# Expert weights on one core: expert 15 takes the third buffer after expert 2, and layer 0's first weights load earlier

## The reference, cut to what matters

```python
def moe(x, r_w, r_b, w1, w3, w2):
    ...
    for e in range(N_EXPERTS):
        h = jax.nn.silu(t @ w1[e]) * (t @ w3[e])
        out = out + gates[:, e:e + 1] * (h @ w2[e]).astype(jnp.float32)

for l in range(DEPTH):
    if l < N_A_LAYERS:
        mix, buf = conv_module(x, conv_past[l], ...)
        conv_new.append(buf)
    else:
        ...
    x = layer_norm(ALPHA * x + mix, ln_mix_g[l], ln_mix_b[l])
    x = layer_norm(ALPHA * x + moe(x, ...), ln_ffn_g[l], ln_ffn_b[l])
```

## Time and profile before

| what | before |
|---|---|
| median of 3 runs | 1090.54 us (1090.39 to 1094.48) |
| profiled execution | 1092.01 us, span 1090.4 us |
| mean granted TensorE clock | 0.936 of 2.4 GHz |
| TensorE busy | 960.4 us, 88% |
| VectorE, ScalarE, GpSimd busy | 338.4, 166.3, 105.3 us |
| moved by DMA | 266.96 MB, 245 GB/s over the span |
| chain that ended last | PE 68%, DMA 12%, DVE 9%, SPq 5% |

### The profile page before, as it was taken

The page is one execution under the profiler, slowest core; times in us unless marked ns, Lnnn a source line. Parts: engine busy times, 40 slices in busy tenths (PEclk is TensorE's granted clock), DMA queues, the critical chain, the costliest instruction groups (busy, mean ns, idle before and its releaser), DMA issues.

```text
span 1090.4 us, 14360 instructions
## 1 busy us (share of the span) xinstructions
PE 960.4 (88%) x4814; PEld 478.6 (44%) x4815; DVE 338.4 (31%) x806; ACT 166.3 (15%) x327; POOL 105.3 (10%) x198
## 2 busy tenths in 40 slices
PE   6979979899989998869998888889798999898993
PEld 4646535444333433326655555444543333333331
DVE  0945454522122211152224433212542121122115
ACT  1000032111111110011123322220111110111101
POOL 0260000101000000013000023000020000000000
PEclk9989989799989999998998989989789999899998
DMA  7974453999979999968203110458468499999981
GB/s 180 258 242 127 122 198 112 354 363 346 367 269 371 378 377 383 395 216 280 69 10 100 52 53 26 167 213 313 135 216 278 174 364 379 384 379 375 384 337 49
DMA packets 131654, 266.96 MB, mean 245 GB/s; under 512 B 7480, under 2 KB 39252, under 8 KB 131585
## 3 DMA queue, kind: packets, MB, share of 16 engines
q1 hardware_dynamic: 121200, 237.74, 62.0%
q10 hardware_dynamic: 5009, 16.15, 4.3%
q0 software_dynamic: 5392, 12.34, 4.1%
HBM read 259.78 MB, written 7.15 MB: 245 GB/s over the span
## 4 chain that ended last, share of the span: by engine, by line
PE 68%; DMA 12%; DVE 9%; SPq 5%; ACT 3%; issue 2%; DVEq 0%; ACTq 0%
PE bank L1004 17%; DMA w<-in_e_w 9%; PE bank L1012 7%; PE bank L897 4%; PE wide L1047 4%; SPq L420 3%; PE bank L788 3%; DMA dbuf<-in_a_w_pw 3%; PE wide L897 3%; PE wide L788 2%; PE wide L1787 2%; PE bank L951 2%; PE bank L804 2%; PE bank L1664 2%; PE bank L1765 2%
## 5 line engine op out<-in xcount | busy, mean ns | idle before, releaser
L1004 PE MATMUL bank<-w,dbuf 128*64 128x512 f32 x960 | 218.9, 609 | 16.4 <-DMA w<-in_e_w 14.9
L1004 PEld LDWEIGHTS bank<-w,dbuf 128*64 128x64 f32 x960 | 75.1, 140 | 155.2 <-issue 155.2
L1012 PE MATMUL bank<-w,dbuf 128*64 128x512 f32 x480 | 115.8, 626 | 11.0 <-DVE dbuf L1438 10.4
L1443 DVE COPY dbuf<-bank 64x512 f32<-64x512 f32 x64 | 44.1, 689 | 159.5 <-PE bank L1012 159.1
L1434 DVE TENSOR_TENSOR dbuf<-dbuf,bank 64x512 f32<-64x512 f32 x32 | 22.1, 690 | 205.1 <-ACT dbuf L707 205.1
L707 ACT ACTIVATE dbuf<-bank 64x512 f32<-64x512 f32 x32 | 18.9, 591 | 410.1 <-PE bank L1004 410.1
L1012 PEld LDWEIGHTS bank<-w,dbuf 128*64 128x64 f32 x480 | 38.6, 143 | 72.8 <-issue 72.8
L1047 PE MATMUL wide<-dbuf,ukT 128*128 128x512 f32 x128 | 62.9, 617 | 3.0 <-DVE dbuf L1443 3.0
L549 POOL COPY idx_col<-idx 64x1 int32 (+1 forms) x32 | 5.7, 179 | 555.6 <-PE bank L951 370.5
L951 PEld LDWEIGHTS bank<-ident,dbuf 64*128 64x128 f32 x448 | 38.9, 160 | 41.4 <-issue 36.8
L536 POOL DMA_DIRECT2D w<-in_cache_kpe x64 | 34.3, 536 | 224.4 <-PE bank L1765 120.6
(11 more groups left out here) (365 smaller groups left out, 1142.7 us busy)
## 6 DMA issues: line engine op xcount, KB each, us to landing
w<-in_e_w SPq DMA_DIRECT2D x90, 2048.0 KB, 20.4
dbuf<-in_a_w_pw SPq DMA_DIRECT2D x16, 512.0 KB, 7.2
w<-u_rows SPq DMA_DIRECT2D x32, 142.0 KB, 3.1
dbuf<-in_a_w_pw ACTq DMA_DIRECT2D x1, 4096.0 KB, 16.8
dbuf<-in_e_w SPq DMA_DIRECT2D x2, 2048.0 KB, 14.8
w<-in_cache_ckv SPq DMA_DIRECT2D x32, 128.0 KB, 2.6
dbuf<-in_cache_ckv SPq DMA_DIRECT2D x32, 128.0 KB, 2.2
dbuf<-in_b_w_o SPq DMA_DIRECT2D x2, 2048.0 KB, 8.5
```

The source lines that it names most:

```text
L1004: last = nc.tensor.matmul(bank[n * C:(n + 1) * C], x[:, k], w[n][k], start=(k == 0), stop=(k == KD - 1))
L1012: last = nc.tensor.matmul(bank[n * C:(n + 1) * C], h[:, k], w[k][:, n * 512:(n + 1) * 512], start=(k == 0), stop=(k == 3))
L1443: last = V.tensor_copy(y_pair[s * C:(s + 1) * C, h * 512:(h + 1) * 512], DOWN[h * C:(h + 1) * C, :])
```

## The change

Loads: the third buffer takes expert 15 as soon as expert 2 is done with it (`third_last`, between the loads of 4 and 5), in both layers; TensorE reads expert 15 from buffer 2 and the counts waited for follow. In layer 0 expert 2's w1 is issued once the gate products are done, the first matrix of expert 1 once the tails are transposed, its w2 once they are stored, all before the projection's end; its w3 and expert 2's dbuf part of w3 at the projection's end. The attention's first weights wait until expert 15's up product has read `dbuf`. Tails: transposed before the projection, in banks 2, 3, 6 and 7, packed by GpSimd after the last gate product, copied and stored by ScalarE behind the Silus; the projection of tiles 1 and 2 waits for those copies.

```diff
--- before.py
+++ after.py
@@ -101,7 +101,7 @@
     MISC = 9 * 16
     SHIFTS, GROUPS, STEPS = 4, 4, 8
     WC = SEQ + 4 * STEPS - 4
-    UB = [7, 4, 5, 7]
+    UB = [2, 3, 6, 7]
     ROUNDS_MAX = DEPTH * 2 * T // H
     OUT_STORES = 10
     PUT_ORDER = [(0, 0), (0, 1), (1, 0), (1, 1), (2, 0)]
@@ -415,25 +415,49 @@
                 src = a["e_w2"][l].rearrange("e (k p) d -> p e k d", p=P)[:, bass.ds(e, 1)]
                 return src.rearrange("p a k d -> p (a k) d")
 
+            def load_half(l, e, s, n):
+                sp.dma_start(part(w13[s], n * KD * FE, KD, FE), w13_rows(l, n, e)).then_inc(w13_ready[s], 16)
+
             def load_13(l, e, s):
                 for n in range(2):
-                    sp.dma_start(part(w13[s], n * KD * FE, KD, FE), w13_rows(l, n, e)).then_inc(w13_ready[s], 16)
+                    load_half(l, e, s, n)
 
             def load_2(l, e, s):
                 sp.dma_start(part(w2[s], 0, 4, D), w2_rows(l, e)).then_inc(w2_ready[s], 16)
 
-            def third_dbuf(l, n):
-                rows = w13_rows(l, n, 2)
+            def third_dbuf(l, n, e=2):
+                rows = w13_rows(l, n, e)
                 sp.dma_start(third_w3a if n else third_w1, rows[:, 0:5] if n else rows).then_inc(w13_ready[2], 16)
 
+            def third_xT(l, n, e=2):
+                if n == 0:
+                    sp.dma_start(third_w3b, w13_rows(l, 1, e)[:, 5:8]).then_inc(w13_ready[2], 16)
+                else:
+                    sp.dma_start(third_w2b, w2_rows(l, e)[:, 3:4]).then_inc(w2_ready[2], 16)
+
+            def third_tok(l, e=2):
+                sp.dma_start(third_w2a, w2_rows(l, e)[:, 0:3]).then_inc(w2_ready[2], 16)
+
             def third_rest(l):
-                w3, w2_all = w13_rows(l, 1, 2), w2_rows(l, 2)
                 sp.wait_ge(r_logit, 3 * (l + 1))
-                sp.dma_start(third_w3b, w3[:, 5:8]).then_inc(w13_ready[2], 16)
-                sp.dma_start(third_w2b, w2_all[:, 3:4]).then_inc(w2_ready[2], 16)
+                third_xT(l, 0)
+                third_xT(l, 1)
                 sp.wait_ge(x_stored, 48 * (l + 1))
                 sp.wait_ge(x_alpha, 3 * (l + 1))
-                sp.dma_start(third_w2a, w2_all[:, 0:3]).then_inc(w2_ready[2], 16)
+                third_tok(l)
+
+            def third_last(l):
+
+                served = sp.value_load(rounds[0:1, 2, 2:3], min_val=1, max_val=ROUNDS_MAX + 1)
+                sp.wait_ge(up_done, E * l + 3)
+                sp.wait_ge(m_up, served)
+                third_dbuf(l, 0, E - 1)
+                third_dbuf(l, 1, E - 1)
+                third_xT(l, 0, E - 1)
+                sp.wait_ge(down_done, E * l + 3)
+                sp.wait_ge(m_down, served)
+                third_xT(l, 1, E - 1)
+                third_tok(l, E - 1)
 
             def load_over(l, e, s, old):
 
@@ -449,25 +473,30 @@
                 sp.wait_ge(cnt_set, l + 1)
                 load_over(l, 3, 0, 0)
                 load_over(l, 4, 1, 1)
+                third_last(l)
                 with sp.Fori(0, (E - 6) // 2) as it:
                     for s in range(2):
                         e = it * 2 + s + 5
                         load_over(l, e, s, it * 2 + s + 3)
-                load_over(l, E - 1, 0, E - 3)
 
             load_13(0, 0, 0)
             load_2(0, 0, 0)
+            sp.wait_ge(h_done, KD)
+            third_dbuf(0, 0)
+            sp.wait_ge(u_turned, 4)
+            load_half(0, 1, 1, 0)
+            sp.wait_ge(u_stored, 32)
+            load_2(0, 1, 1)
             sp.wait_ge(mix_done, 3)
-            third_dbuf(0, 0)
+            load_half(0, 1, 1, 1)
             third_dbuf(0, 1)
-            sp.wait_ge(u_turned, 4)
-            load_13(0, 1, 1)
-            sp.wait_ge(u_stored, 32)
             sp.wait_ge(xg_ready[0], 16)
             sp.wait_ge(xg_ready[1], 16)
-            load_2(0, 1, 1)
             third_rest(0)
             load_rest(0)
+            served = sp.value_load(rounds[0:1, 2, E - 1:E], min_val=1, max_val=ROUNDS_MAX + 1)
+            sp.wait_ge(up_done, E)
+            sp.wait_ge(m_up, served)
             sp.dma_start(wkv[:, :, 0:KV], a["s_w_dkv"].rearrange("(k p) n -> p k n", p=P)).then_inc(ld_kv, 16)
             sp.dma_start(wkv[:, :, KV:], a["s_w_kr"].rearrange("(k p) n -> p k n", p=P)).then_inc(ld_kv, 16)
             sp.dma_start(wdq, a["b_w_dq"][0].rearrange("(k p) n -> p k n", p=P)).then_inc(ld_q, 16)
@@ -517,7 +546,6 @@
 
             pool.wait_ge(glu_done, KD)
             pool.wait_ge(state_set, 1)
-            pool.wait_ge(z_done, 1)
             nc.gpsimd.tensor_copy(u_samp.rearrange("p k (b s) -> p k b s", b=DB),
                                   ext_s[:, :, :, CS:EXTS])\
                 .then_inc(u_packed, 1)
@@ -629,6 +657,7 @@
                 act.wait_ge(nrm_done, j + 1)
                 nc.scalar.activation(acc[:, j], acc[:, j], ACT.Silu, scale=vec_T[:, 24 + j:25 + j],
                                      bias=vec_T[:, 32 + j:33 + j]).then_inc(z_done, 1)
+            copy_tails(act)
             act_experts(act, 0)
             act_attention(act)
             act_experts(act, 1)
@@ -688,8 +717,6 @@
                     nc.scalar.activation(xT[:, 4 * q:4 * q + 4, t0:t0 + m], src, ACT.Copy).then_inc(xT_copied, 1)
                 if i == 0:
                     act_norm(act, 2 * l, 2)
-                if i == 1 and l == 0:
-                    copy_tails(act)
             act.wait_ge(r_aff0, l + 1)
             for i, (t0, m) in enumerate(TILES):
                 act.wait_ge(r_logit, 3 * l + i + 1)
@@ -848,6 +875,7 @@
             conv(7)
             add_channels(6)
             add_channels(7)
+            turn_tails(pe)
             pe.wait_ge(pw2_ready, 16)
             pe_experts(pe, 0, acc, pw2, z_done)
             pe_attention(pe)
@@ -868,6 +896,7 @@
 
         def turn_tails(pe):
 
+            pe.wait_ge(glu_done, KD)
             for q in range(2):
                 for k in range(4):
                     last = nc.tensor.transpose(B[UB[q]][0:CS, k * P:(k + 1) * P], ext[:, 4 * q + k, SEQ:EXTP],
@@ -876,8 +905,6 @@
             for q in range(2):
                 if q == 0:
                     pe.wait_ge(u_packed, 1)
-                else:
-                    pe.wait_ge(u_copied, 1)
                 for k in range(4):
                     last = nc.tensor.transpose(B[UB[q + 2]][0:NS, k * P:(k + 1) * P],
                                                u_samp[:, 4 * q + k], ident[:])
@@ -908,13 +935,15 @@
 
             pe.wait_ge(ld_misc, MISC)
             mix(0)
+            if l == 0:
+                pe.wait_ge(u_copied, 2)
             mix(1)
             turn_tile(pe, r, 2 * l, 0)
+            if l == 0:
+                pe.wait_ge(u_copied, 4)
             mix(2)
             turn_tile(pe, r, 2 * l, 1)
             logits(0)
-            if l == 0:
-                turn_tails(pe)
             turn_tile(pe, r, 2 * l, 2)
             logits(1)
             logits(2)
@@ -1082,7 +1111,7 @@
                     pass
 
             n = 16 * (E // 2) * l
-            n1, n0 = 16 * 8 * l, 16 * 7 * l
+            n1, n2 = 2 * 16 * 7 * l, 16 * 7 * l
 
             p0 = E // 2 * l
 
@@ -1108,13 +1137,13 @@
             to_slots(DOWN[0:H, 0:E * MORE], hot_rest,
                      lambda n, m: right_rest[0:m, n].rearrange("p q e -> p (q e)")).then_inc(r_product, 1)
             turn(g0, 0, n + 16)
-            expert(0, 0, 0, 2 * n1 + 32, n1 + 16, n + 16, 0)
-            expert(1, 1, 1, 2 * n0 + 32, n0 + 16, n + 32, 0)
-            expert(2, 0, 2, 48 * (l + 1), 32 * (l + 1), n + 32, 1)
+            expert(0, 0, 0, n1 + 32, n2 + 16, n + 16, 0)
+            expert(1, 1, 1, n1 + 32, n2 + 16, n + 32, 0)
+            expert(2, 0, 2, 96 * l + 48, 64 * l + 32, n + 32, 1)
             with pe.Fori(0, (E - 4) // 2) as it:
-                expert(it * 2 + 3, 1, 0, it * 32 + (2 * n1 + 64), it * 16 + (n1 + 32), it * 16 + (n + 48), it + 1)
-                expert(it * 2 + 4, 0, 1, it * 32 + (2 * n0 + 64), it * 16 + (n0 + 32), it * 16 + (n + 48), it + 2)
-            expert(E - 1, 1, 0, 2 * n1 + 256, n1 + 128, None, E // 2 - 1)
+                expert(it * 2 + 3, 1, 0, it * 32 + (n1 + 64), it * 16 + (n2 + 32), it * 16 + (n + 48), it + 1)
+                expert(it * 2 + 4, 0, 1, it * 32 + (n1 + 64), it * 16 + (n2 + 32), it * 16 + (n + 48), it + 2)
+            expert(E - 1, 1, 2, 96 * l + 96, 64 * l + 64, None, E // 2 - 1)
             put_rows(p0 + E // 2 - 1, stop=True)
 
 
```

## The result

| | median | runs | range |
|---|---|---|---|
| before, beside it | 1090.47 us | 4 | 1089.82 to 1094.48 |
| changed | 1104.89 us | 4 | 1099.71 to 1107.03 |

The ratio of the changed kernel's time to that of the kernel before is 1.0117 (95% interval 1.0086 to 1.0149): some 12.8 us slower, and 1104.89 us is outside my range of 1086 to 1103. The profiled execution took 1099.71 us (span 1098.1), the shortest of the four. The same kernel later gave 1.0116 [1.009, 1.0141] in six runs, with a profiled span of 1105.3.

What follows compares the result with a forecast made beforehand. TensorE is busiest, but from some expert on in each layer's loop the DMA engines' weight loads set the pace. Expert 5's wait, 4.0, plus layer 1's 0.5 gave +4.5 us on the median 1090.54: 1095.0 us, range 1086 to 1103.

Steps and rivals of the forecast that it cites:

- Load 15 costs expert 5's wait: Layer 0: expert 15's load ahead of expert 5's makes expert 5's up product wait 4 us, bounds 0 and 8.
- My alternative for missing early loads: Layer 0: if early loads are issued late, load 3 finds the old queue; wait 10 to 14 us, 1103.
- Passed on in full through load 7: Layer 0: expert 5's wait delays load 7's issue and every landing behind it equally, so +4.0 us.
- Clock 0, bounds +2.9 and -2.9: Layer 0, expert 5: low clock after the wait +2.9 us, against a faster extra round -2.9; taken as 0.
- The gain that I set against it: Layer 0: expert 5's extra round, 6.55 us before, may run at full clock when moved, -2.9 us.
- Layer 1, +0.5 (-1.8 to +3.5): Layer 1: load 15 mostly fills the idle stretch, load 5 starts 3 to 4 us late, slow start saved; net +0.5.
- Early loads, tails, attention's first weights, 0: Layer 0's early loads, moved tail transposes and the attention's later weights are covered; 0 each, tails ±2.2, weights at most +2.
- The signs that I had named: After-profile: expert 5 waits 2 to 6 us, low clock behind, load 7 at 313 or later, no wait at 15.
- Layer 1's waits: Sign: layer 1 still waits at experts 7, 8, 11 and 12, within 1 us or two of old places.
- The wait is long and cold: Rival: expert 5 waits 8 us, low clock adds 2.9, layer 1 adds 2; 1103 us, chance 0.19.
- The lead is enough: Rival: loads 3, 4 and 15 take 16 us each, expert 5 does not wait; 1090.5 us, chance 0.27.
- faster: Rival: the expert loops' weight waits shrink; 1071 us if all go, realistically 1083; chance 0.12.

Runs made afterwards that it cites:

- e1: The changed kernel again, unaltered, for a second profile; ratio to the kernel before 1.0116 [1.009, 1.0141].
- e5: The changed kernel with expert 15 still in the third buffer but loaded last in both layers; ratio to the kernel before 1.0015 [0.9994, 1.0036].
- e6: The changed kernel with expert 15 loaded behind expert 4 in layer 0 only, last in layer 1; ratio to the kernel before 1.0086 [1.0052, 1.012].
- e7: The changed kernel with expert 15 loaded behind expert 4 in layer 1 only, last in layer 0; ratio to the kernel before 1.0007 [0.9987, 1.0028].
- e3: The kernel before with only expert 15's early load, without the early loads and moved tails; ratio to the kernel before 1.0161 [1.0127, 1.0196].
- e9: The kernel before once more, unaltered, for a second profile; ratio 1.0007 [0.9984, 1.0029].
- e2: The changed kernel with expert 15 back in its old place, early loads and tails kept; ratio to the kernel before 1.0012 [0.999, 1.0034].
- e10: The kernel before with TensorE's code for experts 3 to 6 written out ahead of the loop, loads unchanged; ratio 1.0044 [1.0021, 1.0067].
- e14: The changed kernel with only part of expert 15 early in layer 0, the rest last, timed a second time; ratio to the kernel before 0.9979 [0.9962, 0.9996].
- e12: The changed kernel with only 3.4 MB of expert 15 behind expert 4 in layer 0, the rest last; ratio to the kernel before 0.9971 [0.9951, 0.999].
- e4: The changed kernel with all three buffers in rotation and six experts in TensorE's loop body; ratio to the kernel before 1.0016 [0.9986, 1.0045].
- e11: The changed kernel with expert 15 loaded behind expert 6 in layer 0, last in layer 1; ratio to the kernel before 1.0093 [1.0065, 1.012].

## Why the prediction was too low

- *Load 15 costs expert 5's wait: right in kind, and in size with some luck.* Predicted 4 us (bounds 0 and 8); 3.87, 3.58 and 4.03 us in three profiles. The weights came at 289.77, 5.4 us after the 284.34 that I had counted from, and TensorE was ready only at 285.90: in this kernel, e1, e5, e6 and e7 expert 0's down product takes 5.35 us, not 3.65. The two misses nearly cancel. My alternative for missing early loads, 10 to 14 us, is e3's 10.83.
- *Passed on in full through load 7: right.* The last columns of the table show it. The waits at 11 to 14 do not shrink to make up for it.
- *Clock 0, bounds +2.9 and -2.9: this is the term that was mis-sized, at +3.2.* The cost was there in all three profiles with a wait of some 4 us: expert 5's up product 8.78 us instead of 7.04 (+1.7), and its further round 5.18, 5.35 and 5.14 us instead of 3.66 (+1.5); in the changed kernel the granted clock was 0.53 from 292 to 294 and 0.50 from 308 to 310. It does not follow from every wait: in e3, after 10.83 us, the up product took 8.49 us and the further round 3.66. The gain that I set against it was not the change's to give: the 6.55 us of the earlier trace rows was one execution of the kernel before; e9, e2, e5, e7 and e10 to e14 ran that round in 3.66. From expert 5's start to load 7 the early-loading kernels without a wait (e5, e7, e12) need 20.2 to 20.3 us, the changed one 23.5. (e9 and e2 need 22.0 but reach expert 5 1.7 us sooner: from expert 0's start to load 7 all five need 94.5, the changed kernel, e1 and e6 101.7 to 101.9.) So layer 0 costs 3.9 + 3.2 = 7.1 us, and from expert 0 to 15 it takes 254.7, 254.3 and 253.8 us against 247.3 in e9 and 246.9 in e5, where I had predicted +4 on the 251.0 of the first profile.
- *Layer 1, +0.5 (-1.8 to +3.5): about right.* Alone it gives 1.0007 [0.9987, 1.0028]. From expert 0 to 15 layer 1 took 254.8 us before, 256.6 in the changed kernel, but 261.5 in e1, where expert 1's further round fell on a granted clock of 0.83 (826 to 846) against 1.00 in the changed kernel's first profile. With 15 early in layer 1 it took 257.8 us in e7 and 255.6 in e3, with 15 last 254.5 to 255.1 in e9, e2, e5 and e6. 15's pieces (issued 856.88) fill the idle stretch of the earlier trace rows: 342 GB/s from 856 to 868 in place of 3. The sum of the waits says little here: 12.9 us in e7's layer 1 and 13.9 in e5's, against 8.4 in e9, all three within 0.15% of the kernel before. My reading, which no run tests, is that TensorE waits more where the DMA engines set the pace and its own work happens to be done sooner.
- *Early loads, tails, attention's first weights, 0: right within what can be measured* (e2 1.0012, e5 1.0015). The attention's first projection still waits 6.14 us for ScalarE, at 494.70, as in the earlier trace rows.
- *The signs that I had named.* Load 7 at 313 or later: 313.29. The low clock behind the wait: yes. No wait at 15: yes, in both layers. Layer 1's waits "within 1 us or two of their old places": no, there were six in place of four, at 6, 7, 8, 10, 12 and 14. The projection at 143.7: 143.07.
- *The rivals.* "The wait is long and cold" had the cold right and the length wrong; its 1103 was the nearest number. "The lead is enough" and "faster" fell with the wait itself.

The sum with the measured terms is 7.1 + 0.8 = 7.9 us, the 0.8 being e7's (0.0007 x 1093), or 10.2 with e6's 9.4 us (0.0086 x 1093) in place of the 7.1; the ratio says 12.8. The interval of the latter, 9.4 to 16.2, holds 10.2 and not 7.9. So the clock term alone, 4.5 + 3.2 = 7.7 us, would still have left the forecast too low. What fills the rest stays open. Single profiles don't settle it: against e9 the span of the changed kernel is 6.0 us longer in its first profile and 13.2 in e1, and of e1's last 7 us 5.0 lie between experts 0 and 15 of layer 1, where expert 1's further round took 6.42 us instead of 3.66, and 1.5 behind them; from expert 15 of layer 0 to expert 0 of layer 1 the two kernels take 339.3 and 342.8 us (before, e9), 341.9 and 342.2 (changed, e1), which is no difference beyond that of the two profiles of the kernel before.

The Trainium skill, HBM Reference, section Specifications (TRN2), has about 425 GB/s for a core that streams alone. The trace does not agree: no stretch here showed it for long, 376 GB/s over 130 us at a DMA share of 1.04 and 391 to 399 over six in e12 and e9. By that figure nothing would have waited; expert 5 did.

## What to carry to other kernels

When the DMA engines pace a stretch, its end follows the moment from which they have no gap: find that load (here 7), and price every edit by how much later its data move. A spare buffer filled early with what is needed last holds up what is needed next. A piece that fits into a gap which the trace shows costs nothing (e12 and e14), and wins little if anything. Before setting a slow patch of the one profile you have against a cost, look whether a second profile of the same kernel has it.

## What the hardware showed that I had not expected

- TensorE's code seems to have a price where the DMA engines are full. The loop of two experts fetched nothing from 350 to 460 us; the body of six fetched 11 packets of 16 KB in the same stretch and had stalls of up to 5.63 us. The Trainium skill, Runtime: NRT & Kernel Launch, section Instruction fetch mechanics, has instructions streamed in 16 KiB blocks, at a cost that is mostly hidden; the block size agrees with the row (1.11 MB in 68 packets), the "mostly hidden" does not hold in e4 and e10, if the stalls are the fetches.
- A stall of TensorE often costs more than it lasts. After the waits of 3.6 to 4 us at expert 5 (changed kernel, e1, e6) and of 2.72 and 4.10 us at experts 7 and 10 in e11, the 32 products took 8.78 us instead of 7.04 to 7.09: 1.7 us more, with the granted clock near 0.5 for part of them (0.53 from 292 to 294 in the changed kernel, 0.50 from 336 to 338 in e11), the lower level. It isn't certain: after 3.81 us at expert 12 in e6 they took 7.09, at a granted clock of 1.00. The granted clock of the ten microseconds from 302, in which expert 5's further round lies, was 0.83 in the changed kernel and 1.00 in e9.
